# Seven value slots, one multiplication and one GpSimd page moved in the order of a fused decoder step

## What is computed

```python
z = x @ w_in                                   # q, k, v, B, C, h
s = einsum(q, k_pages) / 8 - slope * distance  # per sample, head and token
p = softmax(s over the 3 best past blocks and the own one)
att = einsum(p, v_pages)
mix = concat(att, B * conv3(C * h)) @ w_out
x1 = layer_norm(2**0.25 * x + mix)
u = conv3(x1 @ w_ffn_up); a, g = split(u)
y = layer_norm(2**0.25 * x1 + (silu(a) * g) @ w_ffn_down)
```

## Time and profile before

| | |
|---|---|
| three executions | 438.18, 438.33, 438.52 us |
| the profiled execution's own time | 437.8 us |
| its span, first to last instruction | 436.0 us |
| mean granted TensorE clock | 0.993 |
| bytes moved over the span | 124.60 MB, mean 286 GB/s |

### The profile page before, as it was taken

How to read it: one execution, slowest core, us unless ns; L and a number is a source line. 1 busy time by engine, 2 the same in 40 slices (tenths; PEclk the granted TensorE clock), 3 DMA queues, 4 the chain that set the end, 5 groups by cost and what they waited for, 6 DMA issues and landing times.

```text
span 436.0 us, 8237 instructions
## 1 busy us (share of the span) xinstructions
PE 412.7 (95%) x2903; PEld 339.2 (78%) x2903; DVE 294.7 (68%) x382; ACT 181.4 (42%) x694; POOL 110.8 (25%) x133
## 2 busy tenths in 40 slices
PE   4999999999999998999999989999999999999990
PEld 4588887876876774765653479999999999999990
DVE  0498999999799976954541275666776776534437
ACT  1587569644469133112110243554455555233201
POOL 1005334995255152200000717122211220000002
PEclk9999999999999999999999999999999999999997
DMA  8999999899999999999999953665556766676002
GB/s 313 397 359 407 405 407 393 316 404 409 409 359 327 338 404 405 406 405 404 402 405 398 318 196 98 194 191 162 158 169 191 213 181 186 183 211 206 3 2 99
DMA packets 109515, 124.60 MB, mean 286 GB/s; under 512 B 5903, under 2 KB 67048, under 8 KB 109466
## 3 DMA queue, kind: packets, MB, share of 16 engines
q1 hardware_dynamic: 101138, 107.30, 70.2%
q10 hardware_dynamic: 8336, 16.78, 10.2%
HBM read 121.65 MB, written 2.61 MB: 285 GB/s over the span
## 4 chain that ended last, share of the span: by engine, by line
PE 64%; DVE 18%; DMA 5%; issue 5%; SPq 4%; POOL 2%; ACT 1%; DVEq 0%; POOLq 0%; ACTq 0%
PE ps L1821 12%; PE ps L1822 11%; PE ps L1823 11%; PE ps L1714 8%; PE ps L1608 6%; DVE qk L939 6%; DVE T L949 5%; PE ps L1437 4%; PE ps L1632 4%; PE ps L1634 3%; PE ps L1384 3%; SPq L360 2%; DMA wring<-in_cache_v 2%; DMA KV<-in_cache_k 2%; POOL x1l L612 1%
## 5 line engine op out<-in xcount | busy, mean ns | idle before, releaser
L1188 DVE TENSOR_TENSOR wlo<-KV,whi 128x2048 fp32r<-128x2048 f32 (+1 forms) x24 | 61.7, 2571 | 57.5 <-ACT whi L838 29.3
L1437 PE MATMUL ps<-xT,wring 128*128 128x264 f32 x384 | 89.6, 388 | 0.1
L1437 PEld LDWEIGHTS ps<-xT,wring 128*128 128x128 f32 x384 | 71.6, 190 | 13.6 <-issue 1.7
L1821 PE MATMUL ps<-x1h,whi 128*128 128x264 f32 x256 | 73.7, 288 | 0.2
L1822 PE MATMUL ps<-x1l,whi 128*128 128x264 f32 x256 | 72.7, 284 | 0.0
L1823 PE MATMUL ps<-x1h,wlo 128*128 128x264 f32 x256 | 72.6, 284 | 0.0
L939 DVE TENSOR_TENSOR qk<-KV,qk 128x1536 f32<-128x1536 f32 (+1 forms) x32 | 67.0, 2097 | 6.6 <-DMA KV<-in_cache_k 2.7
L669 ACT ACTIVATE qk<-qk 128x64 f32<-128x64 f32 x216 | 51.9, 245 | 29.1 <-POOL qk L560 23.1
L949 DVE TENSOR_REDUCE T<-qk 128x24 f32<-128x1536 f32 (+1 forms) x32 | 58.4, 1827 | 0.0
L1821 PE MATMUL ps<-fh,whi 128*128 128x264 f32 x176 | 50.4, 286 | 0.1
L1822 PE MATMUL ps<-fl,whi 128*128 128x264 f32 x176 | 50.0, 284 | 0.0
(11 more groups left out here) (215 smaller groups left out, 574.0 us busy)
## 6 DMA issues: line engine op xcount, KB each, us to landing
KV<-in_cache_k SPq DMA_DIRECT2D x128, 256.0 KB, 6.2
KV<-in_w_ffn_up SPq DMA_DIRECT2D x32, 512.0 KB, 4.7
KV<-in_cache_v SPq DMA_DIRECT2D x60, 256.0 KB, 7.3
wring<-in_cache_v SPq DMA_DIRECT2D x56, 256.0 KB, 6.4
KV<-in_w_ffn_down SPq DMA_DIRECT2D x8, 1408.0 KB, 6.3
wring<-in_w_in ACTq DMA_DIRECT2D x5, 2048.0 KB, 14.0
zbuf<-in_cache_v SPq DMA_DIRECT2D x12, 256.0 KB, 5.3
zbuf<-in_w_ffn_up SPq DMA_DIRECT2D x3, 1024.0 KB, 10.2
```

Source lines behind the costliest of these rows:

```text
L1188: nc.vector.tensor_tensor(wlo[s][:, 0:n], w2[s][:, 0:n], whi[s][:, 0:n], ALU.subtract).then_inc(s_lo, 1)
L1437: ins = nc.tensor.matmul(ps[:, z_bank(n), 0:R], tile[k], xT[:, k, :], start=k == 0, stop=k == KT - 1)
L1821: nc.tensor.matmul(out, wh[k], xh[k], start=k == 0, stop=False)
```

## The change

Four things move; nothing is added or taken away. Line numbers of the changed kernel are two or three higher from the places of the edits on.

1. On TensorE value slots 1 to 6 stand one mixing tile earlier, and slot 7 stands ahead of `mix_tile(7)`.
2. In SP's queue value 9 stands behind key slot 7.2 and quad 1.
3. On VectorE `multiply(20)` stands ahead of `denominators(0)`.
4. On GpSimd the page of slot 17 stands ahead of the fourth conv tile.

```diff
@@ sync @@
             load_values(8, ids_v)
-            load_values(9, ids_v)
             load_keys(7, 2, ids_k)
             load_quad(1)
+            load_values(9, ids_v)
             load_keys(7, 3, ids_k)
@@ gpsimd @@
             for t in range(4):
+                if t == 3:
+                    multiply_page(17)
                 pool.wait_ge(s_ze, 12 + t + 1)
...
-            multiply_page(17)
             multiply_page(18)
@@ vector @@
             reduce(18)
+            multiply(20)
             denominators(0)
             sample_weights(0)
             sample_weights(1)
-            scan(19)
+            reduce(19)
@@ tensor @@
             values(0, 0)
+            values(0, 1)
             mix_tile(0)
+            values(0, 2)
             mix_tile(1)
-            values(0, 1)
+            values(0, 3)
             mix_tile(2)
-            values(0, 2)
+            values(1, 0)
             mix_tile(3)
             pe.wait_ge(s_ctail, 1)
             first_row_tile(0)
-            values(0, 3)
+            values(1, 1)
             mix_tile(4)
             first_row_tile(1)
             first_row_tile(2)
-            values(1, 0)
+            values(1, 2)
             mix_tile(5)
             first_row_tile(3)
             sample_outputs(0)
-            values(1, 1)
             mix_tile(6)
             first_row_tile(4)
-            values(1, 2)
+            values(1, 3)
             mix_tile(7)
             first_row_tile(5)
             first_row_tile(6)
-            values(1, 3)
             first_row_tile(7)
```

## The result

The changed kernel took 440.04 us (median of 20 executions, 438.16 to 443.89), the kernel before 437.75 (20, 437.12 to 438.52). The ratio over all executions is 1.0057, 95% interval 1.0043 to 1.0071: 2.5 us slower; the two medians alone differ by 2.3. The forecast was 437.8, range 437.2 to 438.9, and 0.5 us sooner than before.

A forecast was written before the change was run, and what follows sets the result against it. TensorE's own work was taken to bound the kernel, with 1.6 us of serial chain and 1.4 us of late loads. 1.4 - 0.3 - 0.6 = 0.5 us sooner gave 437.8 us, range 437.2 to 438.9.

The forecast's parts named there:

- The page of slot 17: GpSimd's page moved ahead of the fourth conv tile: taken as 0, bounds -0.1 and 0.3 us.
- The 1.4 us of waits for loads: TensorE's three waits for value slots, near the end of 126.80 to 239.40 us: at most 1.4 us to gain.
- The stream's bound: Loads at value 20, gated by value 14 on TensorE: can land only 1.5 us sooner, less TensorE's delay.
- The hole at value 4: Loads slow at 134 to 142 us behind value slot 1: would close, putting the stream 2.2 us ahead.
- rival C: Nothing arrives: the loads' lead is lost at value 20, time 438.3 us; chance 0.15.
- slots 5 and 6: Value slots in the mixing stretch: landing 0.2 and another 0.6 us late, 0.8 us in all, bounds 0 and 3.9.
- Cover of the last residual: Value slot 7 no longer hides residual 7 before the last row transpose: costs 0.3 us, bounds 0.2 to 0.5.
- `multiply(20)` (0.6 us, by a held L591): VectorE's product of slot 22 holds GpSimd's last conv work, delaying TensorE's first value slot: 0.6 us, bounds 0 and 0.8.
- rival D: Slower: slots 5 and 6 not there when the mixing stretch asks; 441.1 us with no lead; chance 0.15.
- value 9: Behind the row transposes: TensorE waits some 1.0 us, covered by the normalised rows' wait; costs nothing, up to 0.5 us.

The follow-up runs named there:

- the filler run: Changed kernel with one more identity matmul, no work for the output, ahead of TensorE's wait for the gate penalties: 439.64 us, ratio 1.0043.
- the order alone: Kernel before with only TensorE's new order of value slots and value 9's new place in SP's queue: 438.95 us, ratio 1.0027.
- releasing the gate: Kernel before with TensorE's new order, value 9's new place, and values 14 and 15 used some 4 us sooner: 437.57 us, ratio 1.0000.
- with slot 7 kept: Kernel before with TensorE's new order and value 9's new place, but value slot 7 at its old place: 438.17 us, ratio 1.0018.
- with the gate released that order: Kernel before with TensorE's new order except slot 7, value 9's new place, and values 14 and 15 used sooner: 436.75 us, ratio 0.9985.

## Why the prediction was wrong

**The page of slot 17: the step that failed is "I take 0, bounds -0.1 and 0.3 us", and it is the largest miss.** The mechanism was named ("a product of VectorE held by it, ahead of the gate penalties") but not worked out. Where GpSimd goes first it is worth 1.2 us at the penalties (TensorE's wait 2.03 against 0.86 us), of which 0.95 is left at the first value slot; where the product goes first, 0.4 and 0.2. In the medians it is 1.5 to 1.6 us, from the edit alone (ratio 1.0036) and from undoing it (1.0057 to 1.0018). The working had asked what the page's place in `KV` sets free and where page 18 goes. It had not laid GpSimd's shifted instructions beside VectorE's, as it did for `multiply(20)`. The rows for it were in the profile of before: the product at 93.94, and the page's 1.27 us put in front of a conv tile that ended at 93.46. The page ends, and the conv tile starts, on the product. That the tie can go either way no row of before could show.

**A low granted clock behind that wait: not foreseen at all.** It costs 2.6 us in 24 matmuls of the profiled execution, in a part of the executions. That the wait sets it off is supported by the filler run, in which the idle time is 1.17 us and no execution has a low mean clock; where in the other executions the clock fell is not known, since only profiled ones show it.

**The 1.4 us of waits for loads: the step that failed is "The stream's bound is 1.5 us less the same delay, since value 20's gate is on TensorE's order. The two are nearly equal, and I take TensorE's."** The hole at value 4 closed as forecast (value 4 issued at 134.62 us and 403 GB/s in 134 to 142 with the order alone), and the stream led by some 2.5 us up to value 19. But value 20's gate stands in TensorE's order, so its issue didn't move (200.97 us with the new order, 199.85 and 200.27 before, of which a part is the executions' own shift). The 1.5 us was the difference of two medians from issue to landing (5.0 - 3.5). What was gained is less.

From value 20's issue to its last landing it is 6.4 us (mean of the seven profiles with the new order and the gate held) against 7.1 (four with the old order and the gate held): 0.7 us. From that issue to value 31's landing nothing clear is left of it: 37.9 to 39.5 us, mean 38.6, against 38.2 to 39.4, mean 38.7. Behind the hole the loads run at 368 and 389 GB/s with the order alone, instead of 403. The 1.4 itself was the longest of four: the profiles with the old order wait 0.7 to 1.4 us for loads from 172 us on (mean 1.0), the seven with the new order and the gate held 0.2 to 1.6 (mean 0.9). A single profile can't size a term like this.

The loss of the lead at value 20 is rival C's mechanism, and releasing the gate takes the loss back (ratio 1.0027 to 1.0000, intervals apart). C's price of 0 net was also too low: with TensorE later by 0.5 us up to the normalised rows, everything behind is later, and the order alone costs 1.2 us in the medians. About 0.5 us of this shows between the first value slot and the normalised rows (44.89 us, before 44.34 and 44.35): 0.3 fit slots 5 and 6, and 0.2 is the net cost of the new places. The remaining 0.7 I can't assign, since profiles of single executions differ by as much.

**Cover of the last residual (0.3 us, bounds 0.2 to 0.5): right, and more to be had than it says.** The wait is 0.30 us in each profile with slot 7 ahead of the tile, and none with it kept, and the changed kernel is 0.24 us longer than before from the first value slot to the normalised rows (44.58 against 44.34). But that is a net figure: slot 7's place costs 0.58 us by itself, and the other six moves give some 0.3 back. The medians step by 0.8 us both times slot 7 was put back.

**`multiply(20)` (0.6 us, by a held L591): right.** A wait of 0.50 us ahead of the first value slot, 0.57 us from penalties to value slot, 0.6 us in the time of the edit alone.

**Slots 5 and 6 (rival D) and value 9.** The prediction's list is short of slot 4, and its rule that a later TensorE cancels these waits holds in the changed kernel (none in the profile, with TensorE 5.6 us late). With the order by itself slots 4 to 6 cost 0.3 to 0.7 us, so a mild form of D is real there; the changed kernel became slower by another way. D's bound of 3.9 us doesn't follow from its landings: 154.3 - 151.3 is 3.0, and taking 1.4 from 3.9 leaves 2.5 and not 2.8. Value 9 decides nothing, as forecast: with slot 7 kept it lands 0.04 us ahead of its use, and the wait for the normalised rows behind it is 1.5 us instead of 1.6, so what it holds TensorE is hidden there.

**The sum.** The forecast was 1.4 - 0.3 - 0.6 = 0.5 us sooner. With nothing clear of the 1.4, 0.3 and 0.6 as forecast, and 1.5 for page 17, it is 2.4 us slower, against 2.5. That agreement is luck: it leaves out the 0.7 us of the order that nothing explains, and the parts don't add exactly. The three edits by themselves have ratios of 1.0036, 1.0027 and 1.0014, 0.77% together, the whole 0.57%. With the intervals' widths this may be chance or waits that cover each other; it stays open.

## What to carry to other kernels

When an instruction of GpSimd is moved, lay its whole shifted sequence beside VectorE's, not only the moved one: a page that ended on the start of a product let the next instruction hold it by 0.6 us in three profiles of four, and a chain that TensorE waits for passes it on. A lead in a stream of loads is worth something only if no later gate stands in the order of the engine that is to profit; look up what frees the next gated place, and move that use with it (here the released gate turned +0.27% into 0). A value slot that hides a short wait of the chain is best left there: keeping slot 7 was worth 0.8 us in the medians twice, and with the gate released that order is 0.15% faster than before (interval up to 0.9998). And a wait of 2 us on a busy TensorE can cost more than its length: with a filler matmul no execution was as long, but only removing the wait gives the rest back.

## What the runs showed of the hardware beyond that

- After 2.03 us of idle time on TensorE the granted clock was 0.50 from 102 to 108 us in one profile, and did not fall behind the same 2.03 us in another. With 1.17 us, behind a filler, it stayed at full in the profile, and the mean clock was 0.990 or more in all 11 executions.
- VectorE's product of two SBUF tiles and GpSimd's two-input instruction came due within 0.01 us in four profiles. In three GpSimd's took its usual 0.74 or 0.75 us and VectorE's 2.36 instead of 1.76; in one VectorE's took 1.76 and GpSimd's 2.35. Neither side always goes first.
- A queue that had run empty at about 201.5 us did not come back to its full rate at once: 286 and 368 GB/s in the two windows from 202 us, where the queue that stayed full moved 403.
